# Expert outputs of an MoE layer: scored rows added to two totals per token in memory, in place of eight plain rows per token

## What is computed

```python
scores = sigmoid(t @ w_router)                      # 512 tokens x 64 experts
... group-limited choice of 8 experts per token ...
wsel = wsel / sum(wsel) * ROUTED_SCALE              # ROUTED_SCALE = 2.5
gate = one weight per chosen (token, expert), else 0
out = (silu(t @ ws1) * (t @ ws3)) @ ws2             # shared expert
for each expert e:
    a = silu(t @ w1[e]) * (t @ w3[e])
    out = out + (a * gate[:, e]) @ w2[e]
x = layer_norm(ALPHA * x + (1 + gate2) * out)
```

## Time and profile before

| | us |
|---|---|
| median of 3 runs | 2006.43 |
| lowest, highest | 1999.59, 2013.11 |
| profiled execution, device time | 2011.6 |
| profiled execution, span of the trace | 2009.8 |

### The profile page before, as it was taken

The page is one execution under the profiler, slowest core; times in us unless marked ns, Lnnn a source line. Parts: engine busy times, 40 slices in busy tenths (PEclk is TensorE's granted clock), DMA queues, the critical chain, the costliest instruction groups (busy, mean ns, idle before and its releaser), DMA issues. The chain is left out here.

```text
span 2009.8 us, 29708 instructions
## 1 busy us (share of the span) xinstructions
PE 1848.4 (92%) x9848; PEld 1275.9 (63%) x9848; DVE 907.5 (45%) x2097; ACT 742.4 (37%) x1913; POOL 649.9 (32%) x796
## 2 busy tenths in 40 slices
PE   2999999988999899999997799999998999999976
PEld 2644444567444688888885346558656888888852
DVE  4677754377313533333345401237444333333453
ACT  2433310255112544444443200134245444444431
POOL 4143300055212474444442340000133744444421
PEclk9799999999999899999998899999998999999988
DMA  9475646491203799999988403200237898999883
GB/s 341 161 273 215 247 151 210 168 335 43 79 11 123 278 334 335 330 328 331 329 293 343 154 28 112 80 17 1 69 112 273 315 328 319 324 342 343 314 313 133
DMA packets 178546, 443.90 MB, mean 221 GB/s; under 512 B 36004, under 2 KB 43540, under 8 KB 178452
## 3 DMA queue, kind: packets, MB, share of 16 engines
q1 hardware_dynamic: 140436, 371.31, 51.6%
q0 software_dynamic: 38016, 71.39, 9.5%
HBM read 419.39 MB, written 90.23 MB: 254 GB/s over the span
## 5 line engine op out<-in xcount | busy, mean ns | idle before, releaser
L1240 ACT ACTIVATE arena<-psum,lncol 128x128 f32<-128x128 f32 x1024 | 371.5, 469 | 423.6 <-PE psum L771 397.4
L793 PE MATMUL psum<-arena 128*128 128x128 f32 x4096 | 501.9, 278 | 0.0
L793 PEld LDWEIGHTS psum<-arena 128*128 128x128 f32 x4096 | 479.2, 193 | 1.0 <-issue 1.0
L805 PE MATMUL psum<-arena 128*128 128x512 f32 x512 | 243.6, 598 | 9.3 <-DVE arena L1829 9.3
L1717 DVE TENSOR_REDUCE destf<-psum 128x3 f32 (+1 forms) x112 | 18.0, 161 | 416.7 <-PE psum L793 399.6
L2148 POOL TENSOR_TENSOR passed<-ones 128x1 f32<-128x1 f32 x256 | 61.1, 239 | 405.2 <-DVE arena L1829 393.8
L557 PE MATMUL psum<-arena 128*128 128x512 f32 x384 | 178.5, 627 | 0.0
L771 PEld LDWEIGHTS psum<-ident,arena 128*128 128x128 f32 x1024 | 123.6, 144 | 74.2 <-issue 65.4
L1829 DVE TENSOR_TENSOR arena<-psum,arena 128x512 f32<-128x512 f32 x256 | 165.7, 683 | 7.8 <-PE psum L805 5.9
L1385 DVE SCALAR_TENSOR_TENSOR arena<-arena,condT 128x512 f32<-128x512 f32 x126 | 150.7, 1196 | 11.7 <-DMA arena<-in_ada_w_dram 7.3
L2164 POOL DMA_INDIRECT arena<-h_rows,idx x128 | 140.5, 1098 | 22.8 <-issue 7.3
(11 more groups left out here) (265 smaller groups left out, 2364.6 us busy)
## 6 DMA issues: line engine op xcount, KB each, us to landing
arena<-in_moe_w_dram SPq DMA_DIRECT2D x384, 512.0 KB
arena<-in_ada_w_dram SPq DMA_DIRECT2D x32, 1024.0 KB, 5.2
arena<-expert_rows SPq DMA_DIRECT2D x14, 2048.0 KB, 13.3
arena<-in_ssm_w_in_dram SPq DMA_DIRECT2D x10, 2048.0 KB, 10.3
arena<-in_ada_w_dram SPq DMA_DIRECT2D x8, 2048.0 KB, 10.8
expert_rows<-arena SPq DMA_DIRECT2D x4, 4096.0 KB, 27.4
arena<-in_ssm_w_out_dram SPq DMA_DIRECT2D x4, 2048.0 KB, 9.4
arena<-in_kv_ada_w_dram SPq DMA_DIRECT2D x4, 1024.0 KB, 5.3
```

The costliest lines, as they stand in the source:

```text
L793: mm = pe.matmul(psum[:, b, 0:P], w[:, k, :], xeT[u % 2][:, k, :], start=(k == 0), stop=(k == KC - 1))
L805: mm = pe.matmul(psum[:, b, :], aT[u % 2], exp_w[u][:, 2, 512 * n:512 * n + 512], start=True, stop=True)
L1240: ins = act.activation(xeT[u % 2][:, k, :], psum[:, b, P * j:P * j + P], ACT.Identity, scale=h_scale(l, k), bias=h_shift(l, k))
```

## The change

Two totals per layer in memory, one for even and one for odd experts, each 512 rows of 1024 floats (`SUMS = 2`). The indirect DMA of `send` now adds its rows to the token's row of the total of its parity (`compute_op=ALU.add`) instead of writing them to a row of their own. So the rows must be weighted beforehand: the table matmul gets five columns, of which two give the token number and three bfloat16 parts give the token's sigmoid score for the expert; DVE multiplies by the slot's score in `rows_out`. The division by the sum of the scores and the factor 2.5 come at the end, once per token (`gsum`). Two sends to the same total must not overlap, so `send(i)` first waits until the send of expert i-2 has landed.

`krank`, the ranks' weights, the diagonals, PE's 80 matmuls per layer, the adds inside the last group, and `over` go. POOL splits the scores into three bfloat16 parts before the loop (`split_scores`). After the loop SP loads two totals of 2 MB in tiles of 512 KB, and DVE adds them (`add_sums`). The zero fill is 4 x 2 MB instead of 4 x 4 MB. The diff, cut:

```diff
-DVE_ROWS = 3
+SUMS = 2
-        part_dram = nc.dram_tensor("expert_rows", [S * TOPK, D], F32, kind="Internal").ap()
+        sum_dram = [[nc.dram_tensor(f"expert_sum{l}{a}", [S, D], F32, kind="Internal").ap() for a in range(SUMS)]
+                    for l in range(2)]
# PE, tables
+                    if e == 0:
+                        pe.wait_ge(split_ready, 2 * (l + 1))
-                        mm = pe.matmul(ps[:, P:P + 3], onehot[e % 4][:, t, :], V[:, t, e, :],
+                        mm = pe.matmul(ps[:, P:P + 5], onehot[e % 4][:, t, :], V[:, t, e, :],
# PE, after the loop
-                for k in range(DVE_ROWS, TOPK):
-                    pe.wait_ge(gdiag_ready, (TOPK - DVE_ROWS) * l + k - DVE_ROWS + 1)
...
-                            mm = pe.matmul(psum[:, 2 * t + n, :], gdiag[T * (k - DVE_ROWS) + t],
-                                           rank[k][:, t, 512 * n:512 * n + 512],
-                                           start=(k == DVE_ROWS), stop=(k == TOPK - 1))
# DVE, route
-                for t in ts:
-                    ins = dve.tensor_tensor_scan(krank[:, t, :], mask[:, t, :], mask[:, t, :], 0.0, ALU.add, ALU.bypass)
...
-                step(dve.tensor_copy(V[:, R, :, 2], krank[:, R, :]))
# DVE, write_table
-                    dve.tensor_reduce(destf[:, one], ps[:, P:P + 3].rearrange("p (e c) -> p e c", c=3), AX,
-                                      ALU.add).then_inc(dest_ready, 1)
-                    dve.wait_ge(dest_ready, at + 1)
-                    dve.tensor_scalar(table[:, one, 0], destf[:, one], float(NOWHERE), None, ALU.add).then_inc(dest_ready, 1)
-                    dve.wait_ge(dest_ready, at + 2)
-                    dve.tensor_scalar(table[:, one, 1], table[:, one, 0], 3, None,
-                                      ALU.logical_shift_right).then_inc(table_ready, 1)
+                    dve.tensor_scalar(table[:, one], ps[:, P:P + 1], ps[:, P + 1:P + 2], float(NOWHERE), ALU.add,
+                                             ALU.add).then_inc(table_ready, 1)
+                    return dve.tensor_reduce(gslot[:, one], ps[:, P + 2:P + 5].rearrange("p (e c) -> p e c", c=3), AX, ALU.add)
# DVE, glu
+                    dve.tensor_copy(gnow[:, u:u + 1], gslot[:, one]).then_inc(gate_ready, 1)
# DVE, rows_out
-                        dve.tensor_tensor(yrow[u % YROWS][:, cols_], psum[:, b, :], g2bc[:, cols_], ALU.mult
-                                          ).then_inc(drained[b], 1)
+                        dve.scalar_tensor_tensor(yrow[u % YROWS][:, cols_], psum[:, b, :], gnow[:, u:u + 1], g2bc[:, cols_],
+                                                 ALU.mult, ALU.mult).then_inc(drained[b], 1)
# DVE, last group
-                            gates_of(u)
                         glu(g, u, last)
-                        if last and u >= SLOTS // 2:
-                            add_row(2 * u - SLOTS)
# DVE, after the loop
+                def add_sums(a, t):
+                    dve.wait_ge(part_in[a][t], 16 * (l + 1))
+                    return dve.scalar_tensor_tensor(SH[:, t, :], part[a][:, t, :], gsum[:, t:t + 1], SH[:, t, :],
+                                                    ALU.mult, ALU.add)
+                settle()
+                dve.wait_ge(base_ready, T * (l + 1))
+                for a in range(SUMS - 1):
                     for t in range(T):
+                        step(add_sums(a, t))
+                when_more(dve, l, more_blocks)
...
                 for t in range(T):
+                    step(add_sums(SUMS - 1, t))
                     statistics(k, t, SH)
# POOL, at the end of mixer_tiles
+                split_scores(l, 0, T - 1)
+                split_scores(l, T - 1, T)
+            def split_scores(l, t0, t1):
+                R = slice(t0, t1)
+                pool.wait_ge(sig_ready, T * l + t1)
+                step(pool.tensor_copy(V[:, R, :, 2], scores[:, R, :]))
+                settle()
+                step(pool.tensor_tensor(rest[:, R, :], scores[:, R, :], V[:, R, :, 2], ALU.subtract))
+                settle()
+                step(pool.tensor_copy(V[:, R, :, 3], rest[:, R, :]))
+                settle()
+                pool.tensor_tensor(V[:, R, :, 4], rest[:, R, :], V[:, R, :, 3], ALU.subtract).then_inc(split_ready, 1)
# POOL, send
+                    if u >= SUMS or l or not isinstance(g, int) or g:
+                        v = (u - SUMS) % SLOTS
+                        pool.wait_ge(y_out[v % YROWS], 16 * (2 * g + (v // YROWS + 1 if u >= SUMS else 0))
+                                     + 16 * (E // YROWS) * l)
                     carrier(u)
-                    pool.indirect_dma_start(out=part_dram,
+                    pool.indirect_dma_start(out=sum_dram[l][u % SUMS],
                                             out_offset=bass.IndirectOffsetOnAxis(ap=idx[u][:, 0:1], axis=0),
                                             in_=yrow[u % YROWS], in_offset=None,
-                                            bounds_check=last_part, oob_is_err=False).then_inc(y_out[u % YROWS], 16)
+                                            bounds_check=last_row, oob_is_err=False, compute_op=ALU.add).then_inc(y_out[u % YROWS], 16)
# SP, after the loop
-                for k in range(TOPK - 1):
-                    until_sent(sp_, l, E - TOPK + k)
...
-                    sp_.dma_start(rank[k], rows_of[k]).then_inc(part_in[k], 16)
-                when_more(sp_, l, more_blocks, over)
-                until_sent(sp_, l, E - 1)
-                for t in range(T):
-                    sp_.dma_start(rank[TOPK - 1][:, t, :], rows_of[TOPK - 1, :, t, :]).then_inc(last_part_in[t], 16)
+                for a in range(SUMS):
+                    if a == SUMS - 1:
+                        when_more(sp_, l, more_blocks)
+                    until_sent(sp_, l, E - SUMS + a)
+                    for t in range(T):
+                        sp_.dma_start(part[a][:, t, :], sum_dram[l][a][TILES[t], :]).then_inc(part_in[a][t], 16)
```

More of the change, by code:

```diff
@@ L153, in trunk @@
         yrow = [view(16 + 4 * i, D) for i in range(YROWS)]
[L154 to L158, removed]
         zero = view(141, 512)
-        part_over = view(95, TOPK, D)
+        part = [view(95 + 16 * a, T, D) for a in range(SUMS)]
         lnrow_moe = [view(80, D), view(84, D)]
-        scores, sel, mask, gate, krank = (view(64 + i, T, E) for i in range(5))
+        scores, sel, mask = (view(64 + i, T, E) for i in range(3))
+        rest = view(67, T, E)
         top8 = view(70, T * EG, 8)
@@ L211, in trunk @@
         grank = sb("grank", [P, T, EG])
-        gk = sb("gk", [P, T, TOPK])
-        gk_over = gsc
         gsum = sb("gsum", [P, T])
-        V = sb("V", [P, T, E, 3], BF16)
-        destf = sb("destf", [P, E])
-        table = view(90, E, 2).bitcast(I32)
+        V = sb("V", [P, T, E, 5], BF16)
+        gslot = view(68, E)
+        gnow = view(68.5, SLOTS + 1)
+        table = view(90, E).bitcast(I32)
         pos1 = view(74.75, T)
-        V1 = view_b(74.5, T, 4)
-        idx = [sb(f"idx{i}", [P, 2], I32) for i in range(8)]
+        V1 = view_b(74.5, T, 8)
+        idx = [sb(f"idx{i}", [P, 1], I32) for i in range(8)]
         passed = sb("passed", [P, SLOTS + 3])
@@ L310, in trunk @@
             "onehot", "dest", "idx", "rows", "turned", "moved", "weights", "up", "silu", "gated", "down", "yrow",
-            "sent", "step", "carried", "over_in", "over_step", "over_added")} for l in range(2)]
+            "sent", "step", "carried")} for l in range(2)]
         idx_ready = sem("idx_ready")
@@ L362, in trunk, with when_more @@
         OVER = (P + 1) * P - 1
-        def when_more(eng, l, blocks, over=None):
+        def when_more(eng, l, blocks):
             eng.wait_ge(most_ready, l + 1)
@@ L372, in when_more @@
                     blocks(stage)
[L373 to L378, removed]
                 with eng.Else():
@@ L836, in unit @@
                         for t in range(T):
-                            mm = pe.matmul(psum[:, 6, 0:3], onehot[0][:, t, :], V1[:, t, 0:3], start=(t == 0), stop=(t == T - 1))
+                            mm = pe.matmul(psum[:, 6, 0:5], onehot[0][:, t, :], V1[:, t, 0:5], start=(t == 0), stop=(t == T - 1))
                         mm.then_inc(done["dest"], 1)
@@ L1728, in experts @@
                     ps = until_filled(dve, ("table", l, e))
[L1729 to L1735 removed]
+                    write_table(e, ps).then_inc(drained[MARK[("table", l, e)][0]], 1)
                     onehot_of(e + 2, e + 2)
@@ L1812, in glu @@
                     dve.wait_ge(filled[b], base[b] + 4 * g + u // 2 + 1)
+                    one = slice(i, i + 1) if isinstance(i, int) else bass.ds(i, 1)
+                    dve.tensor_copy(gnow[:, u:u + 1], gslot[:, one]).then_inc(gate_ready, 1)
                     if not last:
@@ L1847, in group @@
                             rows_out(g - 1, SLOTS - 1)
-                        if last and u >= SLOTS // 2:
-                            add_row(2 * u - SLOTS + 1)
```

(7 more changed lines are left out.)

176 lines of the change are left out of this document (29 added, 147 removed).

## The result

The changed kernel is slower: 2074.19 us (median of 4 runs, 2072.8 to 2080.04) against 2009.77 us of the kernel before (median of 4 runs: the three of the table above and a fourth). The ratio is 1.033, 95% interval 1.0275 to 1.0383. The forecast was 1956 us, the range 1940 to 2015: wrong in sign.

What follows compares the result with a forecast made beforehand. PE was taken to bound the steady loops, with the gain at their ends: 5.3 + 7.4 (last groups) + 18.3 + 17.8 (ends) + 1.4 (ahead of the loop) = 50.2 us off 2006.4, giving 1956 us, range 1940 to 2015.

Steps and rivals of the forecast that it cites:

- What bounds the kernel: Steady loops: PE sets the pace, 6.31 us an expert, DMA engines close behind at 92%; the loops' ends are loose.
- The scatter's own size: Expert loop: the added read costs up to 0.70 us, DMA demand 6.51 against 6.31 us an expert; hidden, cost 0.
- The cover: Expert loop: weights issued 8 experts ahead, some 50 us, hide an excess building up to 11 us a layer.
- The rival of the DMA bound: Expert loop: DMA engines become the bound, prefetch unused; 22 us of the gain go, 1978 us; chance 0.14.
- The rule weighed in that rival: Scatters in the loop: a reducing DMA reads two sources through one ring, about half of a copy's rate.
- The new wait: POOL's `send`: scatter i waits for i-2; landing expected at 9.1 us where 12.6 us are allowed, so no wait.
- a sign of being wrong: Steady loop: the prediction is wrong if the scatter releases POOL's `carrier`, or PE waits for gathered rows or weights.
- the rival in which it binds a little: POOL's `send` in the loop: landing L from 12.6 to 14 us, time 1972 to 2026 us; chance 0.10.
- The last group and the end: DVE's stall goes, gaining 5.3 and 7.4 us; last scatter to statistics takes 18.1 us, gaining 18.3 and 17.8.
- The term for `when_more`: DVE between last scatter and statistics: two value loads and two branches, now exposed, 1.3 us (0.3 to 3).
- After the statistics: Layer norm tiles: DVE's chain per tile keeps its length, two adds of 683 ns becoming one of 1277; no cost.
- Ahead of the loop: Before the first gather: `krank` gone and first table shorter gain 0.7 us a layer; `split_scores` hidden by 5 us.

Runs made afterwards that it cites:

- four totals: Changed kernel with four totals per layer (`SUMS = 4`) and slots in order, so a scatter waits for the fourth before it: 2086.24 us (one run).
- the spread kernel: Changed kernel with each expert's slots filled in the partition order 0, 8, ..., 120, then 4, 12, ..., then the rest: 1959.11 us, ratio 0.9747 to the kernel before.

## Why the prediction was wrong

**What bounds the kernel.** Right that PE sets the pace of the loops and that the ends are loose. Wrong in what it made of the 92% DMA share: it is a mean over 16 engines that don't carry the same. By the packet sums above, the lower-half engines stood at 6.1 of 6.31 us already (an estimate, and a low one).

**The scatter's own size, the step that failed.** The size was right: 0.70 us forecast, 0.76 measured. What was done with it was not. It was spread over 16 engines (6.51 us of demand, 0.20 too much) when nearly all of it falls on eight, where it counts twice. The lower half comes to 7.3 us an expert by packet sums. Measured it is a little more: from the first gap on (796 us in layer 0, 1690 us in layer 1) PE's turnings of rows come 7.67 and 7.52 us apart in the mean of 43 experts, for 6.35 before it. That is 57 and 50 us, which is the whole excess of the two loops over the forecast. Some of the 0.2 to 0.4 us between sum and pace may be time that packets of the two queues cost each other on one engine; that stays open.

**The cover.** "It is hidden: SP issues weights 8 experts ahead" failed with it. A lead of 50 us covers an excess of 0.2 us for 56 experts, 11 us. It does not cover 1.0 to 1.3 us for 56 experts, 56 to 73 us. Nor were the 50 us all to be had: with the slots in order the last recorded mark of an expert's weights came about 22 us after their last issue already in the kernel before. Some 20 experts in, the lead was used up, and from then on PE went at the pace of the slower engines.

**The rival of the DMA bound** named the right place and had the wrong price, 22 us, and the wrong sign for the kernel: worked out from the same mean. With the loops' measured +93.6 us in place of the forecast -12.7, the sum of the prediction comes to 2062 us, 12 short of what was measured. The range of 1940 to 2015 was bounded by that mean too.

**The rule weighed in that rival.** The Trainium skill (Collectives: The Full Stack, "The bandwidth ceiling: the fold count and why AG ≠ RS ≠ AR") says that a reducing transfer comes out at about half of a copy's rate. The trace agrees: 327 for 160 ns a packet. That two reads through one ring are the reason, no run here shows.

**The new wait.** Forecast not to bind. In the changed kernel it held POOL 16 times, 39.7 us in all, which the prediction had named as a sign of being wrong; but it cost PE nothing that shows (four totals), and in the spread kernel it never held POOL. The price of the rival in which it binds a little was summed wrongly: by the prediction's own formula a landing of 14 us costs 124 x 0.69 = 86 us and the time is over 2040 us, not 2026. Landings in the changed kernel are longer than the forecast 9.1 us only by little, 9.2 us in the middle and 12.5 at most by the semaphore records, in engines that were overloaded.

**The last group and the end.** Right. In the spread kernel the last group runs without the DVE stall, and the loops are 5.9 and 9.2 us shorter than before, for 5.3 and 7.4 forecast. From the last scatter to the statistics 18.1 us were forecast and 15.6 and 15.2 came: the loads of both totals had landed sooner. The term for `when_more`, 1.3 us, had no row behind it; the whole gap of DVE at that place was 0.50 and 0.23 us. The gain there was 20.8 and 20.7 us, not 18.3 and 17.8.

**After the statistics** I had written that DVE's chain per tile keeps its length, since two adds of 683 ns become one of 1277. It did not: the operand moved from PSUM to SBUF, and beside POOL's sum such an add took 3.27 us, 4 us a layer. This was costed at nothing; layer 1's stretch from there on grew by 4.3 us.

**Ahead of the loop.** `split_scores` was hidden as forecast (POOL ended it at 655.7). The gain of 0.7 us was not seen: the first turning came at 671.8 for 671.5, and POOL's `carrier` and copy took up to 0.7 us each there. The first turning lies between 670.3 and 677.1 us in all these runs, so a gain that small can't be told.

The forecast of 1956 us comes near the 1959.11 of the kernel whose scatters are dealt evenly, but in part by luck: there the loops and ends gained 15.1 and 43.6 us for 12.7 and 36.1 forecast, and the stretches after the statistics lost 7.5 us that were forecast as nothing.

## What to carry to other kernels

Before a transfer is called hidden, ask which DMA engines carry it: a partly filled tile whose rows lie in neighbouring partitions loads half of the engines, and a mean share of 0.9 can hide eight that are always busy. If the fill is partial, deal the rows over the partitions; here it made a 3.3% loss a 2.5% gain. And an excess that a prefetch should absorb must be multiplied by the number of rounds and compared with the lead, for the worst engine and not for the mean.

## What the runs showed of the hardware

- An adding scatter's 4096-byte packet took 327 ns for 160; POOL's queue rose from 9.5% of 2009.8 us to 13.9% of 2072.3. The instruction on POOL took 1606 ns in the mean for 1025, which lay hidden.
- SP's issue of a DMA took up to 8.1 us (1.1 in the middle) in the kernel whose weights came late, for 2.0 (0.38) before: a load's lead can be limited at its issue and not only by the buffers.
- With the same work, only the order of the slots changed, the kernel before had the last mark of an expert's weights about 22 us after their last issue (in order) or 6.7 us (spread).
- PE went without a gap at a mean DMA share of 1.01, and starved at 0.89.
- A DVE add with both tiles in SBUF took 3.27 us for 1.28 beside POOL's elementwise sum of 1024 columns; two adds of 512 columns with one operand in PSUM took 1.28 us together there.
